# S5 chunk kernels and outputs on column groups of the array, in two and four PSUM tiles instead of eight

## The reference, cut to what matters

```
bu_re = einsum("blgp,gnp->blgn", ug, bbar_re)        # 32 groups of 16 channels, 64 complex states each
bu_im = einsum("blgp,gnp->blgn", ug, bbar_im)
h = associative_scan(a * h_prev + bu)                # complex, diagonal
y = einsum("blgn,gpn->blgp", h_re, c_re) - einsum("blgn,gpn->blgp", h_im, c_im)
y = y + d_skip * uf
z = gelu(y);  out = z * sigmoid(z @ glu_w + glu_b)
```

## Time and profile before

| | us |
|---|---|
| median of 3 runs | 2038.46 (2036.25 to 2042.24) |
| profiled execution, its own time | 2041.88 |
| its span | 2039.9 |
| PE busy | 1903.0 (93%) |
| DVE busy | 1566.1 (77%) |
| ACT busy | 1171.5 (57%) |
| POOL busy | 381.9 (19%) |

### The profile page before, as it was taken

How to read it: one execution, slowest core, us unless ns; L and a number is a source line. 1 busy time by engine, 2 the same in 40 slices (tenths; PEclk the granted TensorE clock), 3 DMA queues, 4 the chain that set the end, 5 groups by cost and what they waited for, 6 DMA issues and landing times.

```text
span 2039.9 us, 31590 instructions
## 1 busy us (share of the span) xinstructions
PE 1903.0 (93%) x11832; PEld 1607.3 (79%) x11832; DVE 1566.1 (77%) x1718; ACT 1171.5 (57%) x1205; POOL 381.9 (19%) x489
## 2 busy tenths in 40 slices
PE   6876999979998977999999999999999999999995
PEld 5775789979998966699977777777777777777774
DVE  7997856766545996566568889888898888888886
ACT  4343354444444443355466777767777677776775
POOL 7986101993000143100000000000000000000000
PEclk8998999989999988999979999999999999999998
DMA  5447726535554747355759999999999999999996
GB/s 175 148 114 112 254 84 191 174 114 181 182 176 156 217 93 173 128 166 182 262 191 359 371 366 368 382 351 379 371 365 376 351 386 366 358 377 360 386 362 239
DMA packets 98098, 527.54 MB, mean 259 GB/s; under 512 B 11863, under 2 KB 13431, under 8 KB 54359
## 3 DMA queue, kind: packets, MB, share of 16 engines
q1 hardware_dynamic: 86167, 488.69, 65.2%
q0 software_dynamic: 10784, 36.50, 8.2%
q10 hardware_dynamic: 1056, 1.08, 0.1%
HBM read 505.69 MB, written 20.54 MB: 258 GB/s over the span
## 4 chain that ended last, share of the span: by engine, by line
PE 77%; DVE 9%; POOL 6%; issue 4%; ACT 3%; DMA 1%; DVEq 0%; ACTq 0%; SPq 0%; POOLq 0%
PE bank L594 23%; PE bank L596 23%; PE bank L595 23%; POOL s5m L1847 3%; DVE zone L1439 2%; POOL work L1847 1%; PE bank L627 1%; DVE s5m_parts L1764 1%; PE bank L939 1%; PE bank L814 1%; PE bank L810 1%; DVE ring_parts L1319 1%; ACT zone_parts L1265 1%; PE bank L894 1%; DVE s5m L1339 1%
## 5 line engine op out<-in xcount | busy, mean ns | idle before, releaser
L1764 DVE TENSOR_TENSOR s5m_parts<-s5m,ring_parts 128x2048 fp32r<-128x2048 f32 x228 | 518.9, 2286 | 74.3 <-ACT ring_parts L1265 73.7
L1319 DVE TENSOR_TENSOR ring_parts<-ring,ring_parts 128x1024 fp32r<-128x1024 f32 x238 | 312.3, 1315 | 219.7 <-ACT ring_parts L998 219.0
L1265 ACT ACTIVATE ring_parts<-s5m 128x2048 fp32r<-128x2048 f32 x228 | 430.8, 1915 | 81.8 <-DMA s5m<-in_experts 76.2
L594 PE MATMUL bank<-uT_parts,ring_parts 128*128 128x264 f32 x1312 | 383.6, 292 | 45.1 <-DVE uT_parts L1336 25.9
L595 PE MATMUL bank<-uT_hi,ring_parts 128*128 128x264 f32 x1312 | 378.0, 288 | 0.0
L596 PE MATMUL bank<-uT_hi,ring_parts 128*128 128x264 f32 x1312 | 377.1, 287 | 0.0
L594 PE MATMUL bank<-s5m_parts,work_parts 128*112 128x512 f32 x896 | 359.0, 401 | 0.1
L998 ACT ACTIVATE ring_parts<-ring 128x1024 fp32r<-128x1024 f32 x238 | 251.3, 1056 | 186.3 <-PE bank L596 162.4
L1764 DVE TENSOR_TENSOR s5m_parts<-s5m,zone_parts 128x2048 fp32r<-128x2048 f32 x112 | 256.0, 2288 | 67.9 <-ACT zone_parts L1265 67.7
L594 PEld LDWEIGHTS bank<-uT_parts,ring_parts 128*128 128x128 f32 x1312 | 252.6, 193 | 52.9 <-issue 46.2
L596 PE MATMUL bank<-ring_parts,work_parts 128*112 128x512 f32 x640 | 253.9, 397 | 0.0
(11 more groups left out here) (315 smaller groups left out, 3126.0 us busy)
## 6 DMA issues: line engine op xcount, KB each, us to landing
s5m<-in_experts SPq DMA_DIRECT2D x340, 1024.0 KB, 6.4
ring<-in_weights SPq DMA_DIRECT2D x238, 512.0 KB, 3.3
work<-in_sret POOLq DMA_DIRECT2D x8, 512.0 KB, 6.9
s5m<-kscr POOLq DMA_DIRECT2D x16, 256.0 KB, 11.2
zone<-in_sret POOLq DMA_DIRECT2D x8, 512.0 KB, 13.8
out_ret_s<-work POOLq DMA_DIRECT2D x8, 512.0 KB, 6.8
out_ret_s<-zone POOLq DMA_DIRECT2D x8, 512.0 KB, 6.4
xT<-in_xT SPq DMA_DIRECT2D x1, 1056.0 KB, 5.1
```

The lines of the kernel that those rows point to most:

```text
L594: pe.matmul(out, left[0], right[1], start=first, stop=False)
L1265: act.activation(high_slot(c), slot(c, s5m), ACT.Copy).then_inc(high_done, 1)
L1319: dve.tensor_tensor(weights(c, ring_parts), weights(c, ring), f32(weights_hi(c)), ALU.subtract).then_inc(low_done, 1)
L1764: dve.tensor_tensor(slot(c, s5m_parts), slot(c, s5m), f32(high_slot(c)), ALU.subtract).then_inc(low_done, 1)
```

## The change

`PAIRED` is gone. kk has two tiles instead of eight: tile g2 holds all 16 pairs of row half g2, pair j = 4 col + x at partitions 32 col to 32 col + 15. y has four tiles instead of eight: tile 2 half + g2 holds eight pairs, j = 8 half + 4 col + x at partitions 64 col to 64 col + 39. The loops are turned so that neighbouring matmuls go to different column groups. ACT makes as many copies as before, of the same sizes, now from partition ranges of a tile, and frees the tile after its last copy. The waits of POOL for kk and of PE for y count two and four tiles.

```diff
-PAIRED = (0, 4, 1, 5, 2, 6, 3, 7)
...
-        o += [((l, "kk", i), 0) for i in PAIRED]
+        add("kk", 2)
...
-        o += [((l, "y", i), 0) for i in PAIRED]
+        add("y", 4)
...
-                for i in range(4):
-                    outs = [open_tile((l, "kk", i)), open_tile((l, "kk", i + 4))]
-                    for x in range(4):
-                        j = 4 * i + x
-                        for r, c in ((0, clr), (1, cli)):
+                outs = [open_tile((l, "kk", g2)) for g2 in range(2)]
+                for x in range(4):
+                    for r, c in ((0, clr), (1, cli)):
+                        for col in range(4):
+                            j = 4 * col + x
                             for g2 in range(2):
                                 lo, hi = 64 * g2, 64 * g2 + 64
-                                mm = pe.matmul(outs[g2][0:GP, x * P:(x + 1) * P], bb[lo:hi, r, j, :], c[lo:hi, j, 0:P],
-                                               start=(r == 0), stop=(r == 1))
-                                if x == 3 and r == 1:
+                                mm = pe.matmul(outs[g2][32 * col:32 * col + GP, x * P:(x + 1) * P], bb[lo:hi, r, j, :],
+                                               c[lo:hi, j, 0:P], start=(r == 0), stop=(r == 1))
+                                if x == 3 and r == 1 and col == 3:
                                     mm.then_inc(mm_done, 1)
...
-                for i in range(4):
-                    outs = [open_tile((l, "y", i)), open_tile((l, "y", i + 4))]
+                for half in range(2):
+                    outs = [open_tile((l, "y", 2 * half + g2)) for g2 in range(2)]
                     for x in range(4):
-                        j = 4 * i + x
-                        o = [out[0:NC + NS, x * P:(x + 1) * P] for out in outs]
-                        for g2 in range(2):
+                        each = [(g2, col, 8 * half + 4 * col + x,
+                                 outs[g2][64 * col:64 * col + NC + NS, x * P:(x + 1) * P]) for g2 in range(2) for col in range(2)]
+                        for g2, col, j, o in each:
                             g = g2 * GJ + j
-                            pe.matmul(o[g2], xin[:, g, 0:NC + NS], toep[:, g, :], start=True, stop=False)
+                            pe.matmul(o, xin[:, g, 0:NC + NS], toep[:, g, :], start=True, stop=False)
                         for r, c in ((0, clr), (1, cli)):
-                            for g2 in range(2):
+                            for g2, col, j, o in each:
                                 lo, hi = 64 * g2, 64 * g2 + 64
-                                mm = pe.matmul(o[g2], hst[lo:hi, r, j, 0:NC + NS], c[lo:hi, j, GP:GP + P],
+                                mm = pe.matmul(o, hst[lo:hi, r, j, 0:NC + NS], c[lo:hi, j, GP:GP + P],
                                                start=False, stop=(r == 1))
...
-                for i in range(8):
+                for i in range(4):
                     pe.wait_ge(*out_of((l, "y", i)))
...
-                for i in PAIRED:
-                    copy_out((l, "kk", i), s5m[0:GP, i * 512:(i + 1) * 512], at((l, "kk", i))[0:GP, :])
+                for g2 in range(2):
+                    key = (l, "kk", g2)
+                    full(key)
+                    for col in range(4):
+                        c = (4 * g2 + col) * 512
+                        last = act.activation(s5m[0:GP, c:c + 512], at(key)[32 * col:32 * col + GP, :], ACT.Copy)
+                    last.then_inc(freed(key), 1)
...
+                for i in range(4):
+                    key = (l, "y", i)
+                    full(key)
+                    for col in range(2):
+                        g = (i % 2) * GJ + (i // 2) * 8 + 4 * col
+                        last = act.activation(yst[0:NC + NS, :, g:g + 4, :].rearrange("c s g q -> c g s q"),
+                                              at(key)[64 * col:64 * col + NC + NS, :].rearrange("c (g s q) -> c g s q", g=4, s=S),
+                                              ACT.Copy)
+                    last.then_inc(freed(key), 1)
...
-                for i in range(8):
+                for i in range(2):
                     pool.wait_ge(*out_of((l, "kk", i)))
```

More of the change, by code:

```diff
@@ L802, in _ @@
                 pe.wait_ge(toep_in, 128 * (l + 1))
-                for i in range(4):
-                    outs = [open_tile((l, "y", i)), open_tile((l, "y", i + 4))]
+                for half in range(2):
+                    outs = [open_tile((l, "y", 2 * half + g2)) for g2 in range(2)]
                     for x in range(4):
-                        j = 4 * i + x
-                        o = [out[0:NC + NS, x * P:(x + 1) * P] for out in outs]
-                        for g2 in range(2):
+                        each = [(g2, col, 8 * half + 4 * col + x,
+                                 outs[g2][64 * col:64 * col + NC + NS, x * P:(x + 1) * P]) for g2 in range(2) for col in range(2)]
+                        for g2, col, j, o in each:
                             g = g2 * GJ + j
-                            pe.matmul(o[g2], xin[:, g, 0:NC + NS], toep[:, g, :], start=True, stop=False)
+                            pe.matmul(o, xin[:, g, 0:NC + NS], toep[:, g, :], start=True, stop=False)
                         for r, c in ((0, clr), (1, cli)):
-                            for g2 in range(2):
+                            for g2, col, j, o in each:
                                 lo, hi = 64 * g2, 64 * g2 + 64
-                                mm = pe.matmul(o[g2], hst[lo:hi, r, j, 0:NC + NS], c[lo:hi, j, GP:GP + P],
+                                mm = pe.matmul(o, hst[lo:hi, r, j, 0:NC + NS], c[lo:hi, j, GP:GP + P],
                                                start=False, stop=(r == 1))
-                                if x == 3 and r == 1:
+                                if x == 3 and r == 1 and col == 1:
                                     mm.then_inc(mm_done, 1)
@@ L1138, in _ @@
                 root((l, "gv", 3), 1.0 / DV)
-                for i in PAIRED:
-                    copy_out((l, "y", i), yst[0:NC + NS, :, 4 * i:4 * i + 4, :].rearrange("c s g q -> c g s q"),
-                             at((l, "y", i))[0:NC + NS, :].rearrange("c (g s q) -> c g s q", g=4, s=S))
+                for i in range(4):
[7 more added lines that the diff above has]
+                    last.then_inc(freed(key), 1)
                 for m in range(KD):
```

## The result

| | before | after |
|---|---|---|
| median, us | 2039.97 (2036.25 to 2045.7, 8 runs) | 2027.55 (2023.2 to 2029.27, 8 runs) |
| profiled execution, its own time | 2041.88 | 2027.36 |
| its span | 2039.9 | 2025.4 |
| granted clock over the span | 0.966 | 0.960 |

The ratio is 0.9934, 95% interval 0.9919 to 0.9948: the change makes the kernel 13.5 us faster (10.6 to 16.5). The predicted gain, 18.0 us, is a ratio of 0.991, and lies outside the interval.

What follows compares the result with a forecast made beforehand. PE bounds the kernel, with y on the chain in both layers and kk off it. 2 x 9.0 = 18.0 us from 2038.46 gives 2020.5; range from 2016 less 1 to rival 1's 2027.7 with 1 us more.

Steps and rivals of the forecast that it cites:

- the y stage: S5 outputs on PE: 8 steps of 1.12 us, 9.0 us instead of 18.0, so 9.0 us less a layer.
- The 0.11 us a group: In y: each matmul group carries 0.11 us beyond its slots, booked as the price of changing the array's division.
- the evictions: ACT's y copies end later; the third chunk's low part lands about 4.7 us after y, 5.8 allowed; cost nothing.
- the banks: With four y tiles fewer in a rotation of seven, the banks needed are free in time; cost nothing.
- what is late next: After y PE is busy from 275 to 301, so an earlier start there moves everything behind it.
- The 31 ns a record of L743: Possible floor on record spacing: kk would take 4.0 us, and y's state groups 0.60, losing 0.3 us a layer.
- rival 1: In y, columns add nothing beside row halves: state groups 1.01 us instead of 0.56, time 2027.7; chance 0.08.
- rival 2: In y, weight loads not covered between column neighbours: 2.3 us a layer, gain 13.4, time 2025.1; chance 0.06.
- 4 (serial tiles): The four tiles run one after another: y 23.3 us a layer, kk 14.3, time 2049.1; chance 0.03.
- Rival 3: PE meets one more stall without a releaser, like layer 1's 4.52 us between si tiles: time 2025.0; chance 0.07.
- 9.0 us carry through in each layer: The whole y saving of each layer reaches the kernel's total time, 18.0 us in all.
- Gain nothing: kk falls to 1.8 to 4.0 us, but PE waits that much longer for DVE's conv steps: no gain.

Runs made afterwards that it cites:

- before_2: The unchanged kernel run again as a control for a second trace: 2043.84 us, ratio 1.0008 against the kernel before.
- y_only: The changed kernel with the kk part undone, y as changed: 2028.57 us, ratio 0.9928 against the kernel before; measured a second time, 2028.16 us, 0.9931.
- after_2: The changed kernel itself run again for a second trace: 2030.34 us, ratio 0.9943 against the kernel before.
- kk_only: The changed kernel with y put back to eight tiles, kk as changed: 2044.70 us, ratio 1.0022 against the kernel before.
- filler: The changed kernel plus 13 overwritten 512-column matmuls a layer while PE waits for DVE after kk: 2027.27 us, ratio 0.992 against the kernel before.

## Why the prediction was right, and where not

**Right: the y stage.** "The stage 8 x 1.12 = 9.0 us instead of 18.0" came out as 9.16 for 18.00, and 17.7 us in two layers for 18.0. The step that carried it, that column groups work fully beside row halves, is what L811 x16 in 0.58 us shows. The 0.11 us a group was right too: 16 groups, 1.8 us of the 9.2, are now that price. The starts place it at the change of line (200 ns to the next start instead of 109, and 30 more in the slot behind). That the division of the array is its cause stays argued, since in y both lines change wherever the division does.

**Right: the evictions, the banks and what is late next.** 4.75 us forecast as 4.7, nothing waiting behind y.

**Right in size, at the low end: kk.** 2.00 us between the bounds of 1.8 and 4.0. The 31 ns a record of L743, which I kept as a possible floor, is none: 128 records in 2.00 us are 16 ns each. A slot of 8 records starts 0.109 us after the one ahead of it, as a slot of 2 did before.

**The rivals.** 1 (columns add nothing) wanted state groups of 1.01 us, 2 (uncovered loads) 0.70, 4 (serial tiles) 1.90; measured 0.58. All three fell on the same row. Beside rival 2 the prediction set a rule of the Trainium skill (TensorE: Matmul & The Clock Gate, Part 3, The mechanism), by which column neighbours of one row group would not cover each other's loads. This trace does not bear it out: 16 loads of the state line, 112 ns each, go with the 16 records into 0.58 us, where 8 took 0.56. Rival 3 (another stall with no releaser, 2025.0) is the one that the profile resembles: no new stall came, but the one that was there took 6.83 and 5.20 us in the two traces of after. With the fast kk it is 6.83, 5.20 and 6.53 us, without it 4.52, 6.42, 4.68 and 4.44: the two sets overlap, and no effect of the change can be read from them. One sum of the chances is off by a hundredth: the forecast and rivals 1 to 3 make 0.95 for faster, not 0.94.

**Luck.** The range holds the result because rival 1 set its slow end. The median, 2027.55, is nearly the 2027.7 of that rival, but for other reasons than its own: its state groups of 1.01 us are 0.58.

**Wrong: "9.0 us carry through in each layer".** The prediction was 2020.5, the median 2027.55, 7.1 us above. Three terms make it up:

1. The base. 2038.46 was the median of 3 runs. The 94 runs of the kernel before in all the comparisons, before_2 among them, have a median of 2040.9: 2.4 us.
2. The term of y, 18.0 for 17.7: 0.3 us.
3. The rest, some 4.4 us: y gives 17.7 and the run times show 13.5 (10.6 to 16.5). All 14 runs of the changed kernel have a mean of 2028.3, the 94 of before 2041.5: 13.2 less, with 1.5 to either side.

Of the third, this much is shown: it is not in the y stage, and not in a wait behind it; and most of it is missing without the kk part as well, as y_only gains 14.4 us by its ratios and 13.6 by the means of all runs (12 runs, 2027.9). One trace of each kernel shows little of it: before_2 and after_2 differ by 16.6 us, before and after by 14.5, a mean of 15.6 against 17.7, and two traces of one kernel differ by 5.1 us (before) and 3.0 (after).

The clocks that are listed for every run show more. 2 x (1 - clock) x span is the time that a run spent at the half clock:

| | runs | us at the half clock, mean | lowest to highest |
|---|---|---|---|
| before | 86 | 142 | 130 to 155 |
| y_only | 12 | 150 | 141 to 158 |
| kk_only | 12 | 158 | 151 to 168 |
| the changed kernel | 14 | 163 | 154 to 171 |

The means are good to 1 to 3 us (95%), so the low clock has grown with either part, beyond scatter. Time in which PE waits anyway costs nothing, and of the 21 us more in the changed kernel some 10 lie in PE's idle before the first head. In the traces PE is busy at the low clock for 90 and 94 us (before), 99 and 102 (y_only), 101 and 97 (after) and 100 (kk_only). Half of the difference, as PE then does half the work, is an estimate of its price: some 4 us in each. That is the size of what y_only and the changed kernel are short, and of what kk_only costs. PE's busy time outside kk and y agrees: against before it is 3.1 to 5.2 us more in the five traces of after, y_only and kk_only, and 1.5 more in before_2. So the step that failed, "carry through", took it that the work behind y costs what it did; it costs some 4 us more at the low clock. Why the low clock has grown is the point left open: no run changes it by itself, and no single stretch of the table carries it.

**Wrong: "Gain nothing" for kk, as a price in both directions.** In the changed kernel it holds as far as can be told: y_only is level with it within the intervals. Alone, on the kernel before, the kk part cost 4.5 us (1.8 to 7.3). A sentence that failed is that a longer idle "can bring the fall forward only into time in which PE waits anyway": it reckons with the start of the low clock, not with its end. In layer 0 of kk_only it lasts to 169, where in before it is over at 166. By the table that is 1.2 to 1.4 us of the 4.5; the rest is not placed.

## What to carry to other kernels

Where small matmuls already use row halves, column groups beside them are worth as much again: a group with twice the records took 0.58 us where it had taken 0.56, in each of 16 groups of each layer; what remains is a price of 0.11 us wherever the two kinds of group meet. First ask whether the stage lies on the chain: the same rewrite made kk 3.6 times as fast and gained nothing. And when a few microseconds of a forecast are missing, trace the unchanged kernel a second time before explaining them, since two traces of it differed by 5.1 us here, and then compare the clocks of all runs, which showed what single traces could not.

## What the runs showed of the hardware that I had not expected

- PE runs 128 small matmul records (64 by 16 weights, 128 columns moved) in 2.00 us when they lie in 2 x 4 tiles of the array, 16 ns a record, though each record is itself 269 ns long and each weight load 93. Slots follow each other 0.109 us apart, with 2 records side by side as with 8.
- The stall with no releaser went away in five kernels of five that moved 8 transfers to another time (to waits of 0.6 to 1.6 us in those whose waits are listed above) and lasted 4.4 to 8.3 us in the eight traces that left them about at their time. It ended 1.3 to 1.6 us after a 16 KB packet of instructions had arrived, in all eight; in filler, where only PE's instructions are more, it stood in another place and ended in the same way.
- The same kernel shows short half-clock spells, each costing about 1.5 us, at different places in different executions (0.83 against 1.00 in the same ten microseconds of work), and keeping PE busy through a wait kept the clock at 1.00 in layer 1 and not in layer 0. The sum of the spells differs between kernels by more than it scatters (142 us before, 163 after).
